# Expert weights with two consecutive rows on a partition, in an encoder of retention, attention and mixtures of experts

## What is computed

```python
def expert_choice_moe(h, router_w, w_gate, w_up, w_down):
    cap = EC_CAPACITY * n_tok // N_EXPERTS           # 2 * n_tok / 16
    aff = jax.nn.softmax((xt @ router_w).astype(F32), axis=-1)
    gates, idx = lax.top_k(aff.T, cap)               # every expert chooses its tokens
    xe = xt[idx]
    hid = jax.nn.silu(jnp.einsum('ecd,edf->ecf', xe, w_gate)) * jnp.einsum('ecd,edf->ecf', xe, w_up)
    ye = jnp.einsum('ecf,efd->ecd', hid, w_down) * gates[..., None].astype(h.dtype)
    y = jnp.zeros((n_tok, D), h.dtype).at[idx.reshape(-1)].add(ye.reshape(-1, D))
```

## Time and profile before

| | us |
|---|---|
| median of 3 runs | 2440.71 |
| lowest and highest run | 2440.15, 2444.47 |
| span of the profiled execution (first to last instruction) | 2439.0 |
| TensorE busy with products | 2353.6 (96%) |
| VectorE busy | 1783.9 (73%) |
| ScalarE busy | 1362.2 (56%) |
| GpSimd busy | 299.5 (12%) |
| moved by DMA | 577.38 MB, mean 237 GB/s |

### The profile page before, as it was taken

The page is one execution under the profiler, slowest core; times in us unless marked ns, Lnnn a source line. Parts: engine busy times, 40 slices in busy tenths (PEclk is TensorE's granted clock), DMA queues, the critical chain, the costliest instruction groups (busy, mean ns, idle before and its releaser), DMA issues.

```text
span 2439.0 us, 34267 instructions
## 1 busy us (share of the span) xinstructions
PE 2353.6 (96%) x12062; PEld 1959.1 (80%) x12062; DVE 1783.9 (73%) x2053; ACT 1362.2 (56%) x1494; POOL 299.5 (12%) x360
## 2 busy tenths in 40 slices
PE   8999999999989999999999999998789999999997
PEld 7888888888768888888878888877578888888876
DVE  7565566465878888888865677765578888888854
ACT  5233233233457777777763555443257777777762
POOL 1000000000111112211111100000111211121011
PEclk9999999999989999999999999998899999999999
DMA  6424333223599999999970534231599999999931
GB/s 236 133 80 137 108 109 126 72 90 103 194 374 395 395 390 389 396 391 393 349 193 17 144 100 112 83 99 61 202 339 388 396 394 390 390 391 394 347 125 43
DMA packets 210973, 577.38 MB, mean 237 GB/s; under 512 B 24384, under 2 KB 65856, under 8 KB 210752
## 3 DMA queue, kind: packets, MB, share of 16 engines
q1 hardware_dynamic: 193584, 526.35, 57.7%
q0 software_dynamic: 17296, 49.83, 8.0%
HBM read 547.80 MB, written 30.43 MB: 237 GB/s over the span
## 4 chain that ended last, share of the span: by engine, by line
PE 90%; DVE 4%; DMA 3%; issue 1%; ACT 1%; POOL 0%; SPq 0%; DVEq 0%; POOLq 0%; ACTq 0%
PE bank L1575 43%; PE bank L1459 40%; PE bank L1396 4%; PE bank L1761 1%; PE bank L1743 1%; DMA rows_normed<-xn_late 1%; DVE d_parts L619 1%; DMA m_x<-rows_normed,idx_t 0%; DMA rows_summed<-m_y,idx_out 0%; DMA resid<-in_x_sample 0%; DMA raw<-in_ret_w_in 0%; ACT d_parts L610 0%; DVE top_i L1988 0%; DMA resid<-rows_summed 0%; DVE m_at L1990 0%
## 5 line engine op out<-in xcount | busy, mean ns | idle before, releaser
L2128 DVE TENSOR_TENSOR w_parts<-wt,w_parts 128x2048 fp32r<-128x2048 f32 x384 | 874.6, 2290 | 135.9 <-ACT w_parts L1157 126.1
L1157 ACT CAST w_parts<-wt 128x2048 fp32r<-128x2048 f32 x384 | 734.3, 1913 | 197.2 <-PE bank L1575 186.3
L1575 PE MATMUL bank<-w_parts,m_xt 128*128 128x512 f32 x2976 | 689.5, 391 | 2.1 <-ACT m_y L1215 2.1
L1575 PEld LDWEIGHTS bank<-w_parts,m_xt 128*128 128x128 f32 x2976 | 556.2, 188 | 117.6 <-issue 2.9
L1459 PE MATMUL bank<-d_parts,xt 128*128 128x512 f32 (+1 forms) x1872 | 383.4, 361 | 4.5 <-DVE d_parts L619 4.4
L1575 PE MATMUL bank<-w_parts,m_hidt 128*128 128x512 f32 x1632 | 384.0, 395 | 2.8 <-DVE m_hidt L2120 2.8
L1459 PEld LDWEIGHTS bank<-d_parts,xt 128*128 128x128 f32 x1872 | 315.9, 190 | 58.4 <-DVE d_parts L619 5.8
L1575 PEld LDWEIGHTS bank<-w_parts,m_hidt 128*128 128x128 f32 x1632 | 306.8, 190 | 66.7 <-issue 3.3
L619 DVE TENSOR_TENSOR d_parts<-raw,d_parts 128x512 fp32r<-128x512 f32 (+1 forms) x168 | 215.6, 1296 | 108.9 <-ACT d_parts L610 108.0
L610 ACT CAST d_parts<-raw 128x512 fp32r<-128x512 f32 (+1 forms) x168 | 183.4, 1107 | 198.9 <-PE bank L1459 195.1
L1459 PE MATMUL bank<-xt,d_parts 128*128 128x256 f32 (+1 forms) x1536 | 284.1, 340 | 5.2 <-DVE d_parts L619 1.9
(11 more groups left out here) (193 smaller groups left out, 2150.4 us busy)
## 6 DMA issues: line engine op xcount, KB each, us to landing
wt<-in_exp_w_gate SPq DMA_DIRECT2D x128, 1024.0 KB, 13.3
wt<-in_exp_w_up SPq DMA_DIRECT2D x128, 1024.0 KB, 12.5
wt<-in_exp_w_down SPq DMA_DIRECT2D x128, 1024.0 KB, 12.7
raw<-in_ret_w_in SPq DMA_DIRECT2D x32, 1024.0 KB, 5.2
raw<-in_na_w_in SPq DMA_DIRECT2D x24, 1024.0 KB, 5.3
raw<-in_ret_w_in SPq DMA_DIRECT2D x32, 512.0 KB, 4.6
raw<-in_ret_w_out SPq DMA_DIRECT2D x16, 1024.0 KB, 5.1
raw<-in_ple_w_gate SPq DMA_DIRECT2D x8, 1024.0 KB, 8.8
```

Source lines behind the costliest of these rows:

```text
L1157: nc.scalar.copy(w_parts[c % RING][:, 0, :], wt[:, place // 2, place % 2 * 2048:place % 2 * 2048 + 2048])\
L1575: last = nc.tensor.matmul(b[:, :], lhs[x][:, 2 * k + j, :], w[:, part, j, f * HALF:(f + 1) * HALF], start=(k == j == 0 and x == part == 0) ...
L2128: v.tensor_tensor(w_parts[c % RING][:, 1, :], wt[:, k // 2, k % 2 * 2048:k % 2 * 2048 + 2048], w_parts[c % RING][:, 0, :].bitcast(F32), AL ...
```

## The change

A load gives partition p two consecutive rows of the matrix, 2p and 2p + 1 of the 256 of its chunk, as one run of 8 KB, in place of rows p and 128 + p as two runs of 4 KB. So row tile j of a chunk now holds every second row of the 256. For the products to stay the same, the columns they meet have to be taken the same way: column tile 2k + j of `m_x` and `m_hid` holds the features 256k + 2p + j, and the stationary tile of each transpose reads 128 elements with a step of two. Nothing else differs: neither the number of instructions, nor their order, nor a wait.

```diff
                 def load(c, n, place=None):
                     place = c if place is None else place
                     w = (exp_w_gate, exp_w_up, exp_w_down)[c // 4]
-                    dst = wt[:, place // 2, place % 2 * 2048:place % 2 * 2048 + 2048].rearrange("p (t f) -> p t f", t=2)
-                    sp.dma_start(dst, block_of(w[l, n], 2 * (c % 4), 2, 0, D)).then_inc(slot_full[place], 16)
+                    rows = w[l].rearrange("n (k p t) f -> n k p (t f)", p=P, t=2)
+                    sp.dma_start(wt[:, place // 2, place % 2 * 2048:place % 2 * 2048 + 2048], rows[n, c % 4])\
+                        .then_inc(slot_full[place], 16)
...
+                def paired(rows, j):
+
+                    return rows[:, :].rearrange("n (k p t) -> n k t p", p=P, t=2)[:, j // 2, j % 2, :]
+
                 def rows(phase, e, n):
 
                     pe.wait_ge(moe_rows[l], at(16, 16, n))
                     for c in range(2):
-                        transposes(phase, f"x{c}", [m_x[:, (4 * c + k) * P:(4 * c + k + 1) * P] for k in range(4)],
-                                   e, CAP)
+                        transposes(phase, f"x{c}", [paired(m_x, 4 * c + k) for k in range(4)], e, CAP)
...
                     for f in range(2):
-                        transposes(f"{phase}{l}", f"h{f}", [m_hid[:, (4 * f + k) * P:(4 * f + k + 1) * P] for k in range(4)],
-                                   i, CAP)
+                        transposes(f"{phase}{l}", f"h{f}", [paired(m_hid, 4 * f + k) for k in range(4)], i, CAP)
```

## The result

The changed kernel takes 2458.78 us (median of 4 runs, 2456.08 to 2460.21) against 2440.57 of the kernel before beside it (4 runs). The ratio is 1.0076, with a 95% interval of 1.0064 to 1.0087: slower by 0.8%, and outside the predicted range. The span of the profiled execution is 2456.2 us, 17.2 more than before.

A forecast was written before the change was run, and what follows sets the result against it. The prediction took TensorE alone to bound the loop, with weights always loaded in time. Its only nonzero term, +1.0 us at the entry of layer 1, added to the median of 2440.71 gave 2441.7 us, range 2437 to 2450.

The forecast's parts named there:

- Transposes: 512 transposes of `m_x` and `m_hid`: stepped load stays hidden under 82 ns each; 0 taken, ends 0 and 17.9 us.
- Rival A: Transposes of both mixtures: the step halves the stationary tile's load speed, 17.9 us more, 2459.6 us; chance 0.12.
- Loads in the loop: Weight loads in the expert loop: 8 KB packets at 329 ns use 11 of 15.9 us to spare; cost 0.
- Gathers and scatters: Row transfers in the expert loop: a gather lands 1.0 us later behind 8 KB packets, unwaited for; cost 0.
- Entry of layer 1: Last store of normed rows before the first gather: delayed by larger weight packets, +1.0 us, bounds -2.8 and +4.9.
- Entry of layer 0: Stores before the first gather: land up to 5.4 us later, just covered by the wait for indices; cost 0.
- B: Expert loop: DMA becomes the bound from 333 ns per packet; 35 us per layer at 359 ns, 2511 us; chance 0.04.
- C: Both layer entries: stores suffer more than summed, +4.9 and about +2 us, 2447.6 us; chance 0.01.
- D: Both layer entries: fewer packets free the queues sooner, layer 1 gains 2.8 us and first gathers speed up, 2433; chance 0.05.
- E: Weight loads: rows still go in 4 KB packets, queues unchanged, 2440.7 us; counted within the forecast's chance of 0.78.

The follow-up runs named there:

- loads_only: Changed kernel with its 8 KB loads, but transposes reading neighbouring columns without the step: 2439.82 us against 2438.66 of the kernel before, ratio 1.0003.
- steps_only: Changed kernel with its stepped transposes, but the loads of the kernel before (two runs of 4 KB): 2458.74 us against 2438.66 of the kernel before, ratio 1.0086.

## Why the prediction was wrong

**Transposes: the step that failed.** The text took the term as 0, between the ends 0 and 17.9 us, because a stationary load of at most 61 ns had 21 ns of room, and "even a load a third longer is hidden". The true value lies near the upper end: 119 ns per load, 16.6 us. The ends, the place, the number of 448 exposed loads, the point of 82 ns from which it decides, and the sign in the trace ("an eight at 0.9 us or more") were right; the choice between the ends was not. No row had a stationary tile with a step. The nearest row priced a load without one, of 16 partitions and not 96, and it showed how much room there was, not what the step would take. The sentence that many products leave the reading "untouched" was about how much of the kernel is safe, which says nothing of this load. Rival A's account, 2459.6 us, is 0.8 us from the measured median. The mechanism is A's; that the number is so near is partly luck, since A has 1.3 us too much for the loads and holds the +1.0 of the entry, which did not come. Its chance of 0.12 was too low, and so was the top of the range, 2450, which cut it in half.

**The page on cachelines.** The Trainium skill, Advanced Engine Details and Errata, section SBUF Cachelines, gives full speed to two hits on a line of 16 bytes; by that rule the prediction's term came out as 0. For the load of a stationary fp32 tile the measurement decides against that use of it: a step of two, with its two hits, costs 119 ns, as much as a step of four with one hit (121), and steps of three and eight (115 and 111) do not follow the number of hits either.

**Loads in the loop: 0.** Right. Measured alone, 1.0003. The time of an 8 KB packet was taken as 329 ns and is 311 from 836 to 842 us in `loads_only`, under the 321 of two small ones in the same stretch before, so the 11 us of margin that the text spent were not used; the landings came earlier, not later.

**Gathers and scatters: 0, later by about 1 us.** Right: 1.3 and 0.6 us later, at no cost.

**Entry of layer 1: +1.0.** It is +0.14, too little to tell from nothing: the last store takes 24.36 us here, 24.15 in `loads_only` and 24.02 in `steps_only`, which has the small packets, against 24.2 before. For the first part the turns by packet held. In the changed kernel 203 packets of the weights stood against 205 of the stores from 1764 to 1768 us, 205 against 202 to 1772, and 96 against 97 to 1774. The end was wrong. The sum let the second half of the stores run alone behind the weights. In fact the stores had two packets and more for each of the weights from 1774 on (208 against 90, then 246 against 43), and the weights ran on beside them: from 1776 to 1782 us 1.23 MB of stores and 0.74 MB of weights moved together, 328 GB/s, where the sum has 1.05 MB alone at 257 to 397. Why the turns change there is not shown. With 311 in place of 329 ns the sum's first part is also 0.9 us shorter. The stretch from 1760 to 1782 us, GB/s in 40 slices, then the queues:

```profile
GB/s 372 447 343 469 387 477 373 440 395 440 388 447 373 477 387 440 373 425 402 388 440 425 454 402 380 440 395 425 321 381 432 335 328 328 365 372 328 320 256 202
...
q1 hardware_dynamic: 913, 6.56, 71.4%
q0 software_dynamic: 1815, 1.98, 28.7%
```

The section Queues, rings and completion order of the Trainium skill's DMA: Bandwidth & Descriptors has the round go by whole packets. The near equal counts from 1764 to 1774 us, at twice the bytes per weight packet, agree with it. The page's packet holds several descriptors; whether the profile's packets are those, no run here shows.

**Entry of layer 0: 0.** Right: the gather starts at 688.95 against 689.03 us.

**The other rivals.** B (the DMA becomes the bound) fell with 311 ns per packet, and 324 over the longer stretch, both under its threshold of 333. C (the entries suffer more) fell with the entries at +0.14 and 0. D (relief at the entries) fell, since the store did not land sooner. E fell with the packet count, down by 98,304.

## What to carry over

A step on the stationary operand is not free because the product above it has room; where short products stand in a row on the critical chain, each load but the first is exposed, and the step has to be priced or moved to where it hides. When a term has ends of 0 and 18 us and no row between them, the choice is a guess and both ends belong in the range with real weight, above all when nothing in the loop waits for what the change improves: then the change can only lose. A load's landing time that falls after a change proves no gain while its consumers never waited for it, and it can fall because the loop became slower.

## What the runs showed of the hardware

- A load of 96 x 128 fp32 as stationary tile of a transpose takes at most 82 ns without a step (at most 61 for 16 x 128) and 111 to 121 ns with one of 2, 3, 4 or 8 elements; of these the step of eight was the cheapest.
- Behind a 512-column product the stepped load is hidden altogether (0.58 us per transpose and two products either way), but spreading short products one by one among long ones costs about 0.04 us for each, step or no step (ratios 1.0084 and 1.009).
- Packets of 8 KB take 311 ns on a DMA engine where two of 4 KB take 321 (324 and 331 over 420 us), and it moves no time here.
- VectorE's write of `m_hid` from PSUM (96 x 512) took 1100 ns in paired order in place of 677. In the same kernel a GpSimd gather issue took 9.37 us in place of 3.36; that the writes cause this is not shown.
